# In both mixtures of experts: the first modulation turn summed one expert later, inner rows' low parts ahead of modulation products, the fourth expert's down in two parts

## What is computed

```python
aff = sigmoid(xt @ router_w)                 # 256 x 16
# one group of 4 experts a row, in it the top 2, weights normalized -> gates (256 x 16)
for e in range(N_EXPERTS):
    h = silu(xt @ w_gate[e]) * (xt @ w_up[e])        # 1024 -> 512
    y = y + gates[:, e:e + 1] * (h @ w_down[e])      # 512 -> 1024
```

## Time and profile before

| | |
|---|---|
| median of 3 runs | 2597.52 us (2591.91 to 2598.08) |
| profiled execution | 2606.41 us, span 2604.6 us |
| TensorE matmuls busy | 2324.0 us, 89% of the span |
| VectorE busy | 1734.3 us, 67% |
| ScalarE busy | 1177.1 us, 45% |
| POOL busy | 228.8 us, 9% |
| read from HBM | 502.31 MB, 193 GB/s over the span |
| chain that ended last | TensorE 41%, VectorE 7%, ScalarE 3% of the span |

### The profile page before, as it was taken

How to read it: one execution, slowest core, us unless ns; L and a number is a source line. 1 busy time by engine, 2 the same in 40 slices (tenths; PEclk the granted TensorE clock), 3 DMA queues, 4 the chain that set the end, 5 groups by cost and what they waited for, 6 DMA issues and landing times.

```text
span 2604.6 us, 34126 instructions
## 1 busy us (share of the span) xinstructions
PE 2324.0 (89%) x13978; PEld 2052.5 (79%) x13978; DVE 1734.3 (67%) x2095; ACT 1177.1 (45%) x1352; POOL 228.8 (9%) x184
## 2 busy tenths in 40 slices
PE   5779899997878899999799896989989989888997
PEld 5667778886656787888699886779989988767997
DVE  2557557887475756888777668667758766466554
ACT  2354335675353334676443465343344344433442
POOL 6002001120200301220000012000000001000000
PEclk9788999998898899999799998989989999988999
DMA  7314668895402866898587432168858754204651
GB/s 198 130 54 166 239 218 289 294 335 208 150 1 89 311 226 217 308 317 311 170 292 262 153 146 93 53 203 294 273 168 293 264 186 146 96 18 143 200 183 65
DMA packets 241291, 505.58 MB, mean 194 GB/s; under 512 B 10351, under 2 KB 104369, under 8 KB 241136
## 3 DMA queue, kind: packets, MB, share of 16 engines
q1 hardware_dynamic: 216128, 417.84, 46.3%
q10 hardware_dynamic: 21456, 77.09, 8.4%
q0 software_dynamic: 3552, 8.47, 1.3%
HBM read 502.31 MB, written 1.05 MB: 193 GB/s over the span
## 4 chain that ended last, share of the span: by engine, by line
PE 41%; DVE 7%; ACT 3%; issue 1%; ACTq 0%; DVEq 0%
PE PS L1026 20%; PE PS L1041 9%; PE PS L867 5%; PE PS L827 3%; DVE WGL L2157 1%; DVE AR L2160 1%; PE PS L1063 1%; DVE X L2157 1%; DVE XN L2157 1%; ACT WGH L1631 1%; PE PS L1437 1%; DVE AR L2157 0%; PE PS L1070 0%; DVE XN L2154 0%; ACT XN L1587 0%
## 5 line engine op out<-in xcount | busy, mean ns | idle before, releaser
L2157 DVE TENSOR_TENSOR WGL<-ring,WGH 128x2048 fp32r<-128x2048 f32 x258 | 598.7, 2327 | 307.9 <-ACT WGH L1631 175.5
L1026 PE MATMUL PS<-XTH,WGH 128*128 128x256 f32 x1408 | 404.4, 287 | 6.6 <-DVE XTL L2157 6.6
L1026 PE MATMUL PS<-XTH,WGL 128*128 128x256 f32 x1408 | 402.4, 286 | 0.0
L1026 PE MATMUL PS<-XTL,WGH 128*128 128x256 f32 x1408 | 402.4, 286 | 0.0
L1026 PEld LDWEIGHTS PS<-XTH,WGH 128*128 128x128 f32 x1408 | 274.4, 195 | 12.2 <-issue 9.1
L1026 PEld LDWEIGHTS PS<-XTL,WGH 128*128 128x128 f32 x1408 | 274.4, 195 | 4.1 <-issue 1.0
L1026 PEld LDWEIGHTS PS<-XTH,WGL 128*128 128x128 f32 x1408 | 274.1, 195 | 0.0
L2157 DVE TENSOR_TENSOR WDL<-ring,WDH 128x1024 fp32r<-128x1024 f32 (+1 forms) x136 | 221.5, 1629 | 60.6 <-ACT WDH L1783 43.8
L1783 ACT ACTIVATE WGH<-ring 128x2048 fp32r<-128x2048 f32 x96 | 183.3, 1912 | 163.7 <-PE PS L1091 103.4
L1631 ACT ACTIVATE WGH<-ring 128x2048 fp32r<-128x2048 f32 (+1 forms) x74 | 138.5, 1876 | 206.8 <-PE PS L849 65.7
L1822 ACT ACTIVATE XN<-PS 128x256 f32<-128x256 f32 x88 | 33.9, 385 | 359.1 <-PE PS L1026 331.3
(11 more groups left out here) (505 smaller groups left out, 5231.0 us busy)
## 6 DMA issues: line engine op xcount, KB each, us to landing
FA<-in_ada_w ACTq DMA_DIRECT2D x144, 512.0 KB, 6.3
ring<-in_moe_w_up SPq DMA_DIRECT2D x64, 1024.0 KB, 7.3
ring<-in_moe_w_gate SPq DMA_DIRECT2D x64, 1024.0 KB, 7.5
ring<-in_moe_w_down SPq DMA_DIRECT2D x64, 1024.0 KB, 6.9
ring<-in_ffn_w_gate SPq DMA_DIRECT2D x44, 1024.0 KB, 5.7
ring<-in_ffn_w_up SPq DMA_DIRECT2D x44, 1024.0 KB, 9.5
ring<-in_ffn_w_down SPq DMA_DIRECT2D x44, 1024.0 KB, 7.1
ring<-in_hyb_w_in SPq DMA_DIRECT2D x10, 1152.0 KB, 6.6
```

Source lines behind the costliest of these rows:

```text
L1026: ins = mm(PS[:, 4 + b, m * T:(m + 1) * T], w_[:, b, w], x_[:, k, :], start=k == 0 and q == 0, stop=k == KD - 1 and q == 2)
L2157: return V.tensor_tensor(out_, x_, y_, op)
```

## The change

The first turn's sum (`mod_sums` on TensorE, `mod_out` on VectorE) leaves expert 2's slot and stands behind the transposes of expert 2, in bank 7, with a new wait of `up_all(3)` for `mod_out` ahead of the tile that overwrites that bank. The second turn is summed in `marks(5)` instead of `marks(4)`; the products at (2, 4) and (2, 5) move behind, so that experts 4 and 5 have two products each and experts 6 and 7 three, one of them at a new place 1 behind `picked_low`. For experts 1 to 3, `hidden_high` and `hidden_low` stand ahead of the split behind the previous expert's second down half, and ahead of the products at places 4 and 5. `marks(3)` goes ahead of the fourth down on TensorE, and ahead of the splits behind it on VectorE. The fourth down's second half goes behind the gate of expert 4, in the order of pieces too, so from the 24th piece (p23) to the 28th (p27) the two orders differ.

```diff
-MOD_SLOTS = (2, 4, 8)
-MOD_POINTS = [(1, at) for at in range(6)] + [(2, 0), (2, 1), (2, 4), (2, 5)] + [(3, at) for at in range(6)] + \
-    [(i, at) for i in range(4, 8) for at in (4, 4)]
+MOD_SLOTS = (2, 5, 8)
+MOD_POINTS = [(1, at) for at in range(6)] + [(2, 0), (2, 1)] + [(3, at) for at in range(6)] + [(4, 4)] * 2 + \
+    [(5, 4)] * 2 + [(i, at) for i in (6, 7) for at in (1, 4, 4)]
...
-        downs = {0: [0], 1: [], 2: [1], 3: [2, 3], 4: []}.get(i, [i - 1])
-        order += [(d, "down", h) for d in downs for h in range(2)]
+        downs = {0: [(0, 0), (0, 1)], 1: [], DENSE - 1: [(DENSE - 2, 0), (DENSE - 2, 1), (DENSE - 1, 0)],
+                 DENSE: [(DENSE - 1, 1)]}.get(i, [(i - 1, 0), (i - 1, 1)])
+        order += [(d, "down", h) for d, h in downs]
...
@@ TensorE: up_all
                                 pe.wait_ge(S("m_h"), units + unit(i - 1, t) + 1)
+                            if i == 3 and h == 0 and t == 1:
+                                pe.wait_ge(S("mod_out"), turn + 1)
...
@@ TensorE: down_all
-                def down_all(i):
+                def down_all(i, halves=(0, 1)):
...
-                    for h in range(2):
+                    for h in halves:
...
@@ TensorE: marks
-                    if i in MOD_SLOTS:
+                    if i >= DENSE and i in MOD_SLOTS:
...
@@ TensorE: slot(2) and slot_read(2)
-                        mod_sums(turn + MOD_SLOTS.index(i), PS[:, 4, 320:320 + AW // P])
...
-                        pe.wait_ge(S("mod_out"), turn + MOD_SLOTS.index(i) + 1)
...
@@ TensorE: moe
                     turned(i, 0)
                     turned(i, 1)
+                    if i == 2:
+                        mod_sums(turn, PS[:, 7, 0:AW // P])
                 gathered(DENSE)
-                down_all(DENSE - 1)
                 marks(DENSE - 1)
+                down_all(DENSE - 1, (0,))
                 for i in range(DENSE, NE):
...
-                    if i > DENSE:
+                    if i == DENSE:
+                        down_all(i - 1, (1,))
+                    else:
                         down_picked(i - 1, 0)
...
@@ ScalarE: moe (experts 1 to 3, then 4 to 7)
                     if i > 1:
                         after(i - 1, "down", 0)
+                    hidden_high(i, 0)
+                    hidden_high(i, 1)
+                    if i > 1:
                         after(i - 1, "down", 1)
                     loads(i, 4)
-                    hidden_high(i, 0)
-                    hidden_high(i, 1)
                     loads(i, 5)
                 picked_high(DENSE)
                 after(DENSE - 1, "down", 0)
-                after(DENSE - 1, "down", 1)
...
                     after(i, "up", 1)
+                    loads(i, 1)
                     picked_high(i + 1)
...
-                    if i > DENSE:
-                        after(i - 1, "down", 1)
+                    after(i - 1, "down", 1)
...
@@ VectorE: marks, and slot_sums taken out
-                    if i in MOD_SLOTS:
+                    if i >= DENSE and i in MOD_SLOTS:
...
-                    slot_sums(i)
...
@@ VectorE: moe (experts 1 to 3, then 4 to 7)
                     if i > 1:
                         after(i - 1, "down", 0)
+                    hidden_low(i, 0)
+                    hidden_low(i, 1)
+                    if i == 2:
+                        mod_out(turn, PS[:, 7, 0:AW // P])
+                    if i > 1:
                         after(i - 1, "down", 1)
                     products(i, 4)
-                    hidden_low(i, 0)
-                    hidden_low(i, 1)
                     products(i, 5)
                 picked_low(DENSE)
+                marks(DENSE - 1)
                 after(DENSE - 1, "down", 0)
-                after(DENSE - 1, "down", 1)
-                marks(DENSE - 1)
...
                     picked_low(i + 1)
+                    products(i, 1)
                     after(i, "gate", 0)
...
-                    if i > DENSE:
-                        after(i - 1, "down", 1)
+                    after(i - 1, "down", 1)
```

More of the change, by code:

```diff
@@ L2655, in products @@
                         mod_product(TURN * turn + m)
-                def slot_sums(i):
-                    if i == 2:
-                        mod_out(turn + MOD_SLOTS.index(i), PS[:, 4, 320:320 + AW // P])
                 for t in range(TT):
```

## The result

The changed kernel takes **2559.19 us** in the median of four runs (2554.78 to 2561.8), beside 2597.8 for the kernel before in the same measurement: a ratio of 0.9852, 95% interval 0.9829 to 0.9875, a gain of 38.6 us (32.5 to 44.4). Measured again with more rounds the ratio is 0.9858 (0.9843 to 0.9873), a gain of 36.9 us (33.0 to 40.8). The forecast was 2563.5, a gain of 34.0. The profiled execution took 2561.8 us, its span is 2560.0.

A forecast was written before the change was run, and what follows sets the result against it. TensorE bounds the kernel, so gains come only where it stands still or runs at its lower clock. Four parts give 17.3 us in the first mixture, 16.7 in the second: 2597.5 - 34.0 = 2563.5 us, range 2555 to 2577.

The forecast's parts named there:

- Part 1: Expert 2, first turn summed later: stop shrinks to some 4.4 us, ended by VectorE's routing-sums copy; 3.7 us per mixture.
- Part 2: Experts 1 to 3, inner rows' low parts earlier: the 1.83 us stop before the fourth down goes; 3.5 us per mixture.
- Part 3: marks(3) ahead of the fourth down: the 4.16 us stop before up 4 shrinks to 0.3; 6.1 us per mixture.
- Part 4: Fourth down in two parts: the 2.33 us stop at marks(4) goes, with 1.1 of clock; 3.5 us per mixture.
- rival B: Expert 2's gate: the shorter stop left there costs no clock; 2559 us, chance 0.07.
- The margin at expert 6: After up 5's start, picked_low(6) ends at 14.1 us and TensorE wants it at 14.4: holds by 0.3 us.
- A: Queues behind the modulation products run late, so the stop before up 4 stays; at worst 2576 us, chance 0.12.
- C: DMA sets the pace in experts 5 to 15, so the time is waited for later; 2597.5 us, chance 0.03.
- D: ScalarE, held at loads, splits pieces late in experts 4 to 7 of both mixtures; slower, 2614.5 us, chance 0.03.
- POOL's hold: One-hots beside m12 and m13: 0 taken for VectorE; by the lock rule 0.6 us each, about 2 us less gain.

The follow-up runs named there:

- copy_early: Changed kernel with VectorE's copy of the routing sums moved ahead of expert 2's first two products and a split: 2551.66 us, ratio 0.9821.
- sums4: Changed kernel with the fourth down whole again ahead of expert 4 and the second turn's sums back in marks(4): 2576.97 us, ratio 0.9916.
- undo3: Changed kernel with marks(3) put back behind the first half of the fourth down: ratio 0.9909.

## Why the prediction was right

**Total.** 34.0 us booked, 36.9 and 38.6 measured, both intervals holding 34.0; in the two mixtures 34.7 and 38.3. Range and sign held, and so did the mechanism at each stop. That the sizes added up so well was in part luck. By place in the first profile after, the first mixture gained 2.8 (part 1), 10.1 (parts 2 and 3) and 3.9 us (part 4), the second 5.4, 8.0 and 4.0, where 3.7, 9.6 and 3.5 were booked for each. The prediction read the clock behind the later stops in the first mixture alone and took the second to be like it (only for the gate did rival B give both). It was not:

```profile
971.03 0.70 PE L1179 MATMUL PS<-WDH,HTH 128*128 128x512 f32 x2 [1.82 <-DVE HTL L2157]
...
982.01 0.50 PE L1236 MATMUL PS<-XN 128*128 128x1 f32 x4
...
986.67 0.47 PE L1091 MATMUL PS<-WGH,XTH 128*128 128x512 f32 x1 [4.16 <-issue]
...
993.83 3.73 PE L1216 MATMUL PS<-XN,X 128*128 128x128 f32 x32
```

These are rows of the kernel before. Behind the stop of 1.82 us the down takes 10.98 us, where 12.59 was booked, and up 4 takes 7.16, where 7.63 was: 2.1 us of clock less to win. The gate behind the first stop lost 1.5 us more there than in the first mixture, which made part 1 worth that much more. The two nearly cancelled.

**Part 1.** Right in its mechanism to the tenth: the copy ends at 291.43 + 0.18 = 291.61 (291.6), the stop is 4.45 us (some 4.4; in the second mixture 5.00 and 5.17, a little above the 4 to 5 forecast), the sums follow the transposes at once, up 3 doesn't wait. The clock loss of the stop, booked at 2.2, was 2.97 and 1.88 in one profile, some 1.5 in each mixture of the other. Booked 7.4 for both mixtures; 6.2 alone and 9.0 left out lie on both sides. That the copy, not m7, holds TensorE there was shown by copy_early and by its lack of effect on the kernel before. Rival B falls: the shorter stop does cost clock.

**Part 2.** The stop went. Booked 7.0, measured 4.5 alone and 9.3 left out. What the sum did not say is that parts 1 and 3 lean on it, and its 1.7 us of clock were not there in the second mixture.

**Part 3.** Booked a stop of 0.3, found none: the gate column is there 0.44 us before TensorE wants it, so the margin that I put at 0 was a little better. Booked 12.2, measured 10.0 alone and 11.3 left out.

**Part 4.** The term that was mis-sized. Booked 7.0; it measured 8.3 alone and 11.6 left out. The step priced the clock by the 24 matmuls of up 5 alone, 1.1 us a mixture. It left out the sums, marks and transposes between the stop and them. At the full level these take 1.71 us (316.27 - 314.56) and 1.22 (from 379.33 to the idle 0.20 before 380.75), 2.9 together; in the rows of before they took 398.23 - 394.68 = 3.55, and in sums4 386.20 - 381.28 = 4.92. With these 0.6 us the rows of before give a clock loss of 1.7 a mixture and 8.1 us for the part, and 8.3 is what it brought alone. In sums4 the lower clock lasted longer behind the same stop. Of sums4's 11.6 us the busy time shows the split:

```profile
292.20:623.10 330.90, 322.94 (x1708) 276.24 (x1708) 246.87 (x183) 196.31 (x155) 42.13 (x24) 0.97 0.79 280
894.90:1225.60 330.70, 322.83 (x1708) 276.36 (x1708) 246.34 (x185) 194.81 (x154) 45.08 (x24) 0.97 0.80 283
```

Its 15.8 us without a matmul are 4.2 more than the changed kernel's 11.6 (booked 4.66), and its 645.8 us busy are 7.4 more than the mean of 640.2 and 636.6 (booked 2.2). So the stop was right, and the clock was sized at two thirds of what the rows of before hold and at under a third of what it was worth in the changed kernel. The margin at expert 6 was forecast as 14.1 against 14.4 us after up 5's start. `picked_low(6)` ended at 394.83 and so 14.08 behind 380.75, and TensorE did not wait. The 0.20 us left before up 5 was not in the sum.

**Rivals.** A: no stop before up 4, and none in experts 5 to 7 but the 0.20 us before up 5. m13's load was late by 0.19 us, and the margin held it. C: in the stretch that answers to experts 5 to 15 TensorE is busy in all 164 us while DMA goes up from 307 to 317 GB/s, so the loads were not the pace. D: from 400 us to the end of each mixture nothing of ScalarE's releases TensorE.

**POOL's hold.** The Trainium skill (SBUF — State Buffer, "SBUF: two separate sides") says that VectorE with two SBUF inputs and a GpSimd instruction that reads SBUF lock one port pair against each other, and by the prediction's estimate that would have cost 2 us. In this order of starts, which no row of before showed, POOL's two one-hot instructions took 2.57 us together, started during VectorE's split (352.57 to 354.86) and during m12, and ended 0.48 and 0.47 us behind the ends of these:

```profile
354.07 1.27 POOL L730 TENSOR_SCALAR XN<-XN 128x128 f32<-128x128 f32 x1 [59.92 <-PE PS L1239]
355.31 1.33 POOL L730 TENSOR_SCALAR XN<-XN 128x128 f32<-128x128 f32 x1
```

m12 took 1.39 us. In undo3, where the one-hots come later, the same product took 1.28. POOL's two waits agree with the lock; the hold of VectorE does not, for it is 0.11 us long and not 0.6. The same 1.39 stands in the second mixture and in the second profile. The 0 that the sum took was nearer.

## What to carry to other kernels

When a wait is taken out of a queue that is worked in order, ask what stands behind it in the *other* engine's queue: here the copy behind m7 kept 4.45 of 7.07 us, and moving it forward brought another 10 us. Read the clock behind a stop at every place where the stop occurs: behind 1.82 and 1.83 us the same 48 matmuls lost 0.1 and 1.7. Price each part of a change both ways, alone and left out; where the two differ, the parts share a cover, and undoing one of them may cost twice its worth. A margin of a few tenths, added up from durations of rows, held here in both mixtures, for blocks at full clock repeat (the 48 matmuls of expert 1's down take 10.88 or 10.89 us in both mixtures of all fourteen profiles). The clock behind a stop does not: in these profiles it cost 1.4 to 3.0 us behind the stops of 2.6 to 5.2 us, and 3.1 to 4.7 behind those of 5.3 to 7.9.

## What was not expected of the hardware

The loss of clock behind the same stop differs between two executions of the same kernel: 36 matmuls behind 4.45 us of stop took 11.14 us, and behind 4.31 us in the other profile 9.66, where 8.2 are due. Nor does it go by the stop's length: behind 2.60 us in sums4 they took 9.88.

A hold of VectorE by POOL that is much longer than the one above was in the trace all along, ahead of the change's stages and the same before and after. POOL adds two SBUF operands there, and a split of VectorE takes 4.47 us in place of 2.29:

```profile
251.22 8.74 POOL L745 TENSOR_TENSOR X<-X,ROWB 128x1024 f32<-128x1024 f32 x2
```

```profile
257.63 4.47 DVE L2162 TENSOR_TENSOR WDL<-ring,WDH 128x2048 fp32r<-128x2048 f32 x1
```

POOL's two instructions end at 259.96 and the split at 262.10, 2.14 later, nearly its whole length when alone: it seems to have run once POOL had finished. The one-hots, which held m12 by 0.11 us, have one large SBUF input instead of two and are shorter as well (128 columns, not 1024), so these rows do not tell which of the two makes the difference.
